# DeltaNet's inverse by levels: where the level masks are put on, and the order of VectorE's work around it

## The reference

```
decay = exp(where(lower_incl, G[..., :, None] - G[..., None, :], -inf))
kb = k * beta[..., None]
a_mat = where(lower_strict, einsum('bhnid,bhnjd->bhnij', kb, k) * decay, 0.0)
rhs = concatenate([v * beta[..., None], kb * exp(G)[..., None]], axis=-1)
sol = triangular_solve(a_mat + eye(C), rhs, left_side=True, lower=True)
u, w = sol[..., :dv], sol[..., dv:]
```

## Time and profile before

| | |
|---|---|
| median of three runs | 2952.0 us |
| profiled execution | 2951.58 us, of which the span of instructions is 2949.8 |
| TensorE products busy | 2918.7 us, 99% of the span |
| TensorE weight loads | 2489.2 us, 84% |
| VectorE busy | 1781.9 us, 60% |
| ScalarE busy | 1499.9 us, 51% |
| DMA | 183 GB/s in the mean, 538.85 MB |
| granted TensorE clock | 0.999 in the mean |

### The profile page before, as it was taken

The page is one execution under the profiler, slowest core; times in us unless marked ns, Lnnn a source line. Parts: engine busy times, 40 slices in busy tenths (PEclk is TensorE's granted clock), DMA queues, the critical chain, the costliest instruction groups (busy, mean ns, idle before and its releaser), DMA issues.

```text
span 2949.8 us, 35566 instructions
## 1 busy us (share of the span) xinstructions
PE 2918.7 (99%) x14328; PEld 2489.2 (84%) x14328; DVE 1781.9 (60%) x2400; ACT 1499.9 (51%) x2337; POOL 8.9 (0%) x10
## 2 busy tenths in 40 slices
PE   8999899999999999999999999999999999999999
PEld 7887888888888889998888888888999888888887
DVE  6877765656555656657664555554855766445554
ACT  6654445555556545555464444445555555444442
POOL 0000000000000000000000000000000000000000
PEclk9999999999999999999999999999999999999999
DMA  9554233665545565555555556555645545656554
GB/s 365 180 186 150 93 115 119 217 228 186 170 159 194 176 204 188 164 169 163 170 171 198 194 191 222 191 186 192 208 142 175 169 160 171 199 188 217 196 186 156
DMA packets 274452, 538.85 MB, mean 183 GB/s; under 512 B 9040, under 2 KB 50128, under 8 KB 272112
## 3 DMA queue, kind: packets, MB, share of 16 engines
q1 hardware_dynamic: 270576, 515.35, 53.1%
q10 hardware_dynamic: 3712, 21.23, 1.8%
HBM read 527.11 MB, written 9.44 MB: 182 GB/s over the span
## 4 chain that ended last, share of the span: by engine, by line
PE 94%; DVE 3%; ACT 1%; DVEq 1%; issue 1%; DMA 0%; ACTq 0%; SPq 0%
PE acc L401 28%; PE acc L403 28%; PE acc L402 28%; PE tb L701 1%; DVE w_lo L364 1%; PE tb L2469 1%; ACT w_hi L346 0%; PE tb L1023 0%; PE tb L2353 0%; PE tb L2341 0%; PE tb L2339 0%; PE tb L1921 0%; PE tb L1906 0%; PE tb L1294 0%; PE tb L2330 0%
## 5 line engine op out<-in xcount | busy, mean ns | idle before, releaser
L364 DVE TENSOR_TENSOR w_lo<-raw,w_hi 128x1024 fp32r<-128x1024 f32 (+3 forms) x1008 | 1139.9, 1169 | 593.2 <-ACT w_hi L346 581.8
L346 ACT ACTIVATE w_hi<-raw 128x1024 fp32r<-128x1024 f32 (+3 forms) x1008 | 985.6, 1015 | 566.4 <-PE acc L403 518.5
L401 PE MATMUL acc<-w_hi,x_hi 128*128 128x512 f32 (+4 forms) x2880 | 1115.8, 387 | 8.6 <-DVE w_lo L364 8.6
L403 PE MATMUL acc<-w_hi,x_lo 128*128 128x512 f32 (+4 forms) x2880 | 1085.5, 377 | 0.0
L402 PE MATMUL acc<-w_lo,x_hi 128*128 128x512 f32 (+4 forms) x2880 | 1083.9, 376 | 0.0
L401 PEld LDWEIGHTS acc<-w_hi,x_hi 128*128 128x128 f32 x2880 | 542.9, 189 | 95.2 <-DVE w_lo L364 8.5
L403 PEld LDWEIGHTS acc<-w_hi,x_lo 128*128 128x128 f32 x2880 | 541.9, 188 | 92.0
L402 PEld LDWEIGHTS acc<-w_lo,x_hi 128*128 128x128 f32 x2880 | 543.2, 189 | 86.0
L401 PE MATMUL acc<-w_hi,mB_hi 128*128 128x512 f32 x256 | 100.6, 393 | 0.0
L403 PE MATMUL acc<-w_hi,mB_lo 128*128 128x512 f32 x256 | 99.7, 390 | 0.0
L402 PE MATMUL acc<-w_lo,mB_hi 128*128 128x512 f32 x256 | 99.6, 389 | 0.0
(11 more groups left out here) (495 smaller groups left out, 3168.7 us busy)
## 6 DMA issues: line engine op xcount, KB each, us to landing
raw<-in_h_w_in SPq DMA_DIRECT2D x184, 1024.0 KB, 5.0
raw<-in_o_w_in SPq DMA_DIRECT2D x56, 1024.0 KB, 5.2
raw<-in_h_w_branch SPq DMA_DIRECT2D x48, 1024.0 KB, 5.1
raw<-in_e_w_in SPq DMA_DIRECT2D x47, 1024.0 KB, 5.1
raw<-in_h_w_out SPq DMA_DIRECT2D x32, 1024.0 KB, 5.1
raw<-in_h_w_in SPq DMA_DIRECT2D x40, 768.0 KB, 4.3
raw<-in_e_w_out SPq DMA_DIRECT2D x16, 1024.0 KB, 5.0
raw<-in_o_w_out SPq DMA_DIRECT2D x16, 1024.0 KB, 5.0
```

Source lines behind the costliest of these rows:

```text
L346: act.activation(k.w_hi[:, a % HI_SLOTS, rows, :width], k.raw[:, a % SLOTS, rows, :width], ACT.Copy).then_inc(k.hi_ready, 1)
L364: e.tensor_tensor(k.w_lo[:, a % SLOTS, rows, :width], k.raw[:, a % SLOTS, rows, :width], k.w_hi[:, a % HI_SLOTS, rows, :width].bitcast(F32 ...
L401: pe.matmul(out, x_hi[:, tok], wh, start=first, stop=False)
L403: mm = pe.matmul(out, x_lo[:, tok], wh, start=False, stop=last)
```

## The change

The levels' masks are no longer multiplied into the system. TensorE multiplies the whole `AT` with `T`; ScalarE copies the product with the factor -1; and at the end of the level VectorE copies, instead of subtracting, the result into `T` (or `U`) only where the level's mask is set (`copy_predicated`, with the same bf16 masks read as 16-bit integers). `Am` is not written any more, and VectorE has nothing to do at even visits 2 to 6.

The order of VectorE's queue changes too: at all odd visits and at v = 0 the fill steps' low parts stand behind the visit; the norms stand behind both; the 16 x 16 blocks of the backward runs are laid at entry 7 instead of 4, and the substitution steps stand at the odd entries 9 to 37 instead of the even ones 6 to 34.

```diff
@@ pe_dn_visit, even visits
-                mm = pe.matmul(X[:, h, :], m.Am[:, h, :], m.T[:, h, :], start=True, stop=True)
+                mm = pe.matmul(X[:, h, :], m.AT[:, h, :], m.T[:, h, :], start=True, stop=True)
@@ act_dn_visit, even visits
-        ins = act.activation(m.Y[:, :, :], X, ACT.Copy)
+        ins = act.activation(m.Y[:, :, :], X, ACT.Copy, scale=-1.0)
@@ dve_dn_visit
-    levels = (k.ms("up")[:, 4 * 128:] if d == 0 else k.ms("down")).rearrange("p (n d) -> p n d", d=128)
-
-    def am(level):
-        return dve.tensor_tensor(m.Am[:, :, :], m.AT[:, :, :], spread_rows(levels[:, level - 1, :], 3), ALU.mult)
+
+    def joined(level, forward):
+        up = (d == 0) == forward
+        n = 4 + level - 1 if up else level - 1
+        mask = k.ms("up" if up else "down")[:, n * 128:n * 128 + 128].bitcast(mybir.dt.int16)
+        return spread_rows(mask, 3)
...
-        am(1)
...
-        if v % 2 == 0:
-            if level < LEVELS - 1:
-                dve.wait_ge(k.dn_y, (LEVELS - 1) * 2 * n + 2 * (level - 1) + b + 1)
-                am(level + 1)
-        else:
+        if v % 2 == 1:
             dve.wait_ge(k.dn_z, (LEVELS - 1) * 2 * n + 2 * (level - 1) + b + 1)
             if level < LEVELS - 1:
-                dve.tensor_tensor(m.T[:, :, :], m.T[:, :, :], Y, ALU.subtract).then_inc(k.dn_am, 1)
+                dve.copy_predicated(m.T[:, :, :], joined(level, False), Y).then_inc(k.dn_am, 1)
...
-                dve.tensor_tensor(m.U[:, :, :], m.U[:, :, :], X, ALU.subtract).then_inc(k.dn_inv, 1)
+                dve.copy_predicated(m.U[:, :, :], joined(level, True), X).then_inc(k.dn_inv, 1)
@@ dve_even
-        late = dn_quota(i) if v <= 1 else 0
+        late = dn_quota(i) if v == 0 or v % 2 == 1 else 0
         dve_fill(k, dve, dn_quota(i) - late)
-        dve_na_norm(k, dve, i)
         dve_dn_visit(k, dve, n, b, v)
         dve_fill(k, dve, late)
-        if i == 4:
+        dve_na_norm(k, dve, i)
+        if i == 7:
             dve_dn_blocks(k, dve, 1)
-        elif 4 < i < 4 + 2 * BLOCK and i % 2 == 0:
-            dve_dn_substitute(k, dve, 1, i // 2 - 3)
+        elif 7 < i < 7 + 2 * BLOCK and i % 2 == 1:
+            dve_dn_substitute(k, dve, 1, i // 2 - 4)
```

## The result

The changed kernel takes 2937.67 us (median of five, 2937.23 to 2937.72), the kernel before 2952.0: a ratio of 0.995, interval 0.9939 to 0.9961. That is 14.3 us faster; 2939.5 was forecast, within 2935.5 to 2945. Five more executions, beside the kernel before again, gave 2937.54, ratio 0.995 (0.9937 to 0.9962). The span of the profiled execution is 2935.9 us, 13.9 shorter than before.

A forecast was written before the change was run, and what follows sets the result against it. A fixed-length TensorE queue, changed only by waits and clock, bounds the kernel. DeltaNet losses fall from 18.9 to 6.4 us, gaining 12.5: 2951.58 becomes 2939.1, or 2939.5 with 0.4 for the median; range 2935.5 to 2945.

The forecast's parts named there:

- The view: DeltaNet stretch: a fixed TensorE queue loses 18.9 us before, 6.4 after; its waits fall from 12.7 to 4 to 5.
- Masks gone: Twenty-four VectorE multiplications of 0.551 us go; TensorE's wait of 0.54 at 280.56 falls to about 0.05.
- Copies under a mask: Twenty-four VectorE subtractions become masked copies, taken at 0.55 us each, ends 0.35 and 0.95.
- Rival (a): A dear masked copy, 0.95 us instead of 0.55: 3.6 us less gain, 2943.1 us; chance 0.15.
- Answer first: Odd visits, copy ahead of low parts: 3.38 us wait at i=8 goes whole; 0.83 of 0.93 stays at second half.
- Norms behind: First run, reduce behind at i=11: the 0.89 us wait goes, a new 0.83 wait on ScalarE's copy comes.
- Second run: Visits i=20 to 41, set by VectorE's queue: 4.1 us lost with tails against 7.7, largest wait 1.56 at i=32.
- State's values, last two runs: Wait of 2.09 us at i=38, 39 goes; 0.28 and 0.27 at i=50, 67 become 0.10 and 0.
- Clock: Two DeltaNet stretches of 3.40 us at 0.50 return to full clock, giving 3.4 us back.
- (b): Second run keeps waits and low clock, 2946.5 us, or only the clock falls twice, 2942.9; chance 0.15 in either form.
- (d): Masked copy so dear VectorE paces all four runs: 2957 us at 2.5 us a copy; chance 0.05 including nearby costs.
- Rival (c): All DeltaNet waits and both low-clock stretches go, VectorE's queue being shorter: 18.9 us gain, 2933.1 us; chance 0.08.

The follow-up runs named there:

- the second copy: Changed kernel with another masked copy, into a tile nothing reads, ahead of each of the 24: 2943.31 us, ratio 0.9971.
- norms ahead: Changed kernel with the norms put back ahead of the visit: 2937.72 us, ratio 0.9954.
- low parts first: Changed kernel with the low parts ahead of the visit at odd visits, as before: 2945.31 us, ratio 0.9979.
- spread steps: Changed kernel with norm reduces ahead of the visit, multiplications behind, and the fifteen substitution steps moved to where TensorE does not wait: 2934.95 us, ratio 0.9942.
- masks-only kernel: Changed kernel's masked copies, without mask multiplications, in the old order of VectorE's queue: 2948.97 us, ratio 0.9988; profiled execution 2943.18 us.
- reduces ahead: Changed kernel with only each norm's reduce ahead of the visit, its multiplication behind: 2938.24 us, ratio 0.9954.
- order alone: Kernel before with the new order of VectorE's queue, keeping mask multiplications and subtractions: 2943.59 us, ratio 0.9973.
- blocks early: Changed kernel with blocks at entry 4 and substitution steps at even entries 6 to 34, as before: 2940.96 us, ratio 0.9963.

## Why the prediction was right

- **The view.** A fixed TensorE queue that loses time in waits and to the clock: lost after by its own account is 3.7 us in seven waits (4 to 5 was the sign), with 0.28 for each tail 5.6; 18.9 less 5.6 is 13.3, and the stretch became 12.9 shorter. The account closes within 0.4. It holds run by run too: 4.5, 7.0 (3.4 of it the clock) and, for the last two, 1.0 us were forecast, 4.75, 6.85 and 1.33 measured. So the number is not luck. The 0.28 a wait has another make-up than the prediction gave: most waits stand behind a fill product, drawn 0.40 at 512 columns and holding TensorE 0.23, so 0.17 is drawn as busy; and the visit behind a wait holds TensorE 0.11 us longer than one that did not wait (0.69 from 291.26 to 291.95, 0.58 from 282.72 to 283.30, in the kernel before).
- **Masks gone.** The wait of 0.54 became 0.07 (0.05 forecast). By themselves they give 3.3 us in the stretch, the clock apart, a quarter of their 13: the sum had followed the queue and did not add 24 times 0.55.
- **Copies under a mask.** Taken as 0.55, measured 0.588 and 0.590. The Trainium skill ("Vector Engine (DVE) Microarchitecture Reference", Anatomy of a single slice) says that the engine has two source streams and no path for three tensors, from which the prediction drew a possible second pass. The rows show none: 0.04 us more, where a pass over 384 elements was worked out at 0.40. Rival (a) falls with it. Its slope of 9 us per 1 us of a copy counted waits alone; the second copy measured 6 by waits and 11 with two falls of the clock, which (a) did not have.
- **Answer first.** The largest term; alone it measured 7.6 us, some 3.7 in waits and the rest by the clock. At entry 8 the copy was forecast to end at 285.61 and ended at 285.46; the 3.38 went whole. At entry 9 the low pair was forecast from 286.92 and the copy to 289.75; they stand at 286.63 and 289.49, and 0.60 stays. The forecast's figures count from where TensorE asks (its 0.93 of before is the row's 0.77 and 0.16 that is drawn as busy), so beside its 0.83 stands 0.77.
- **Norms behind.** The new wait on ScalarE came, 0.64 in the row, 0.81 from where TensorE asks, for 0.83. ScalarE in order of time, against the earlier trace rows:

```profile
298.62 0.30 ACT L584 ACTIVATE stat<-stat,const_cols 128x8 f32<-128x8 f32 x1 [4.77 <-DVE stat L1214]
...
299.10 0.47 ACT L1084 ACTIVATE dn<-tb 128x384 f32<-128x384 f32 x1
```

  ScalarE stands 4.77 us for the reduce with its own copies queued behind the root (3.55 before). The edit gives back what it takes: with the norms ahead, the time is the same.
- **Second run.** Forecast 0.40, 0.20, 0.74, 0.48, 1.56 and 0.14; the rows have 0.33, none, 0.49, 0.21, 1.34 and none: 2.4 us, 3.5 with tails, for 4.1. From where TensorE asks, as the forecast counts, they are 0.49, none, 0.65, 0.46, 1.50 and none, 3.1 for 3.5. The largest stands where it was put, at entry 32.
- **State's values, last two runs.** The 2.09 went, and comes back with low parts first (2.1). Runs three and four gained 0.3 and 1.03 us, 1.3 together, for 1.0.
- **Clock.** Both stretches came back at full clock, 3.4 us, in the profiled execution, and the mean of all ten is 1.000. That the length of a wait alone does not tell, which the prediction said, is shown below.
- **What was not in the sum.** 1.0 us outside the stretch: 0.3 ahead of it, where the traces start by up to 1.3 us apart from kernel to kernel (269.96 to 271.28), and 0.64 behind, most of it attention waits (4.61 to 4.20 us). It makes, with the 0.4 in the stretch, the 1.4 by which the profiled span came out shorter than forecast. The last 0.4 of the 1.8 us between 2939.5 and 2937.67 was added for a median above the profiled execution; here the two agree (2937.67 and 2937.72).

Rivals (b) and (d) are refuted by the same rows: no wait over 1.34, no half clock, 0.59 a copy. Rival (c), all waits gone, is not what the change does; its size is what the spread steps reach in the stretch (4.24 us more), so the waits that were left were a matter of place too.

## What to carry to other kernels

Where an engine works through one queue for two customers, list for each of its answers what stands ahead of it in the queue, work that itself waits above all; take that order before the amount of work. Here 13 us of work taken away brought 3.3 us in the stretch and a changed order 5.4, the clock apart (2.7 and 8.0 in the medians). Count a gain in waits together with the clock: the parts nearly add in the stretch, and by the mean clocks only both together kept TensorE at its upper level in every execution.

## What the runs showed of the hardware

- A copy under a mask of 128x384 out of PSUM, mask in 16-bit integers, takes 0.59 us, the subtraction of this shape 0.548.
- One wait does not always bring the clock down. Behind waits of 2.7 us (289) and 2.35 us (332) the masks-only kernel's profiled execution kept 1.00; low parts first, with 2.65 us at the same place, has a stretch at 0.50 right behind; the wait of 1.84 in the attention has 0.50 right behind it in the profiled executions of four kernels (the second copy, norms ahead, reduces ahead, steps spread anew) and 1.00 in those of six (before, changed, masks alone, order alone, low parts first, blocks early). Executions of one kernel differ too, by their mean clock (0.999 in four of five, 1.000 in one, with the steps spread anew). So the length of a wait does not decide by itself; what else does, stays open.
- A fall costs 1.7 us by its row (3.40 us at the 1.2 GHz level). Executions of one kernel with a mean clock of 0.999 and of 1.000 lie 1.3 us (2941.0 and 2939.7, blocks early) to 2.5 us (2935.0 and 2932.5, steps spread anew) apart, which fits but says no more: ten executions of the changed kernel, all at 1.000, spread over 1.9 us.
